# A hybrid encoder layer in which the first product starts block by block, neighbourhood attention takes two heads at a time, and the ends of two stages are rearranged

## The reference, cut to what matters

```python
h = rms_norm(x, norm_g)
dq, dk, dv, nq, nk, nv, gates = jnp.split(h @ w_in, IN_SPLITS, axis=-1)
y_diff = diff_attention(...)            # (p1 - lam * p2) @ v, per head, with a shared bias
y_na = neighborhood_attention(nq, nk, nv, rpb)   # per head and query: its window of keys, a bias per head
x = x + (g_diff * (y_diff @ w_br_diff) + g_na * (y_na @ w_br_na)) @ w_out
aff = softmax(rms_norm(x, norm2_g) @ w_router)
gate, idx = lax.top_k(aff.T, cap)       # 32 prompt and 64 sample tokens per expert
y = x + scatter_add((silu(xe @ wg) * (xe @ wu)) @ wd * gate)
```

## Time and profile before

| | us |
|---|---|
| median of 3 runs (2209.09 to 2210.94) | 2210.21 |
| the profiled execution | 2212.8 |
| its span, as the profile shows it | 2211.0 |
| PE busy in the span | 2128.8 (96%) |
| DVE busy | 1582.0 (72%) |
| ACT busy | 1370.8 (62%) |
| POOL busy | 238.7 (11%) |
| mean granted clock of TensorE | 0.987 |

### The profile page before, as it was taken

The page is one execution under the profiler, slowest core; times in us unless marked ns, Lnnn a source line. Parts: engine busy times, 40 slices in busy tenths (PEclk is TensorE's granted clock), DMA queues, the critical chain, the costliest instruction groups (busy, mean ns, idle before and its releaser), DMA issues.

```text
span 2211.0 us, 27257 instructions
## 1 busy us (share of the span) xinstructions
PE 2128.8 (96%) x10388; PEld 1592.4 (72%) x10388; DVE 1582.0 (72%) x1249; ACT 1370.8 (62%) x1102; POOL 238.7 (11%) x137
## 2 busy tenths in 40 slices
PE   6999999999968999999999999999999999999997
PEld 5867888887756767777677776767767677777765
DVE  5374363233456888888888888888888888888885
ACT  5364364122225777777777777777777777777764
POOL 2202120000130001010101102011010201101010
PEclk9999999999988999999999999999999999999999
DMA  5111141113436999999999999999999999999995
GB/s 232 58 36 67 58 144 60 64 58 115 162 118 236 373 370 366 376 371 385 364 368 385 367 378 370 373 373 370 378 365 380 365 374 385 367 376 374 375 372 184
DMA packets 71389, 623.97 MB, mean 282 GB/s; under 512 B 8272, under 2 KB 8656, under 8 KB 18608
## 3 DMA queue, kind: packets, MB, share of 16 engines
q1 hardware_dynamic: 63264, 595.62, 69.6%
q0 software_dynamic: 7648, 27.40, 4.4%
q10 hardware_dynamic: 432, 0.34, 0.0%
HBM read 609.70 MB, written 13.63 MB: 282 GB/s over the span
## 4 chain that ended last, share of the span: by engine, by line
PE 82%; DMA 7%; DVE 6%; ACT 4%; issue 1%; POOL 0%; ACTq 0%; SPq 0%; DVEq 0%; POOLq 0%
PE PS L527 25%; PE PS L529 25%; PE PS L528 25%; DMA x_w_raw<-in_w_expert_gate 5%; DVE x_w_low L1160 4%; ACT x_w_high L1090 3%; PE PS L625 2%; PE PS L610 2%; PE PS L872 1%; DMA x_w_raw<-in_w_expert_up 1%; PE PS L638 1%; PE PS L536 1%; PE PS L815 1%; PE PS L736 0%; DMA cst<-in_consts 0%
## 5 line engine op out<-in xcount | busy, mean ns | idle before, releaser
L1160 DVE TENSOR_TENSOR x_w_low<-x_w_raw,x_w_high 128x2048 fp32r<-128x2048 f32 (+1 forms) x382 | 1174.5, 3086 | 241.9 <-ACT x_w_high L1090 239.6
L1090 ACT ACTIVATE x_w_high<-x_w_raw 128x3072 fp32r<-128x3072 f32 (+1 forms) x384 | 980.0, 2558 | 266.2 <-PE PS L529 190.9
L527 PE MATMUL PS<-x_w_high,xT_high 128*96 128x512 f32 (+1 forms) x1536 | 580.5, 378 | 9.7 <-DVE x_w_low L1160 7.6
L529 PE MATMUL PS<-x_w_high,xT_low 128*96 128x512 f32 (+1 forms) x1536 | 575.4, 375 | 0.0
L528 PE MATMUL PS<-x_w_low,xT_high 128*96 128x512 f32 (+1 forms) x1536 | 573.4, 373 | 0.0
L527 PEld LDWEIGHTS PS<-x_w_high,xT_high 128*96 128x96 f32 x1536 | 248.3, 162 | 105.6 <-DVE x_w_low L1160 18.6
L529 PEld LDWEIGHTS PS<-x_w_high,xT_low 128*96 128x96 f32 x1536 | 248.1, 162 | 90.0
L528 PEld LDWEIGHTS PS<-x_w_low,xT_high 128*96 128x96 f32 x1536 | 248.8, 162 | 85.1 <-issue 0.2
L527 PE MATMUL PS<-x_w_high,hidden_high 128*96 128x512 f32 x704 | 281.3, 400 | 0.0
L529 PE MATMUL PS<-x_w_high,hidden_low 128*96 128x512 f32 x704 | 276.7, 393 | 0.0
L528 PE MATMUL PS<-x_w_low,hidden_high 128*96 128x512 f32 x704 | 275.9, 392 | 0.0
(11 more groups left out here) (185 smaller groups left out, 1774.4 us busy)
## 6 DMA issues: line engine op xcount, KB each, us to landing
x_w_raw<-in_w_expert_gate SPq DMA_DIRECT2D x96, 1536.0 KB, 8.4
x_w_raw<-in_w_expert_up SPq DMA_DIRECT2D x96, 1536.0 KB, 8.8
x_w_raw<-in_w_expert_down SPq DMA_DIRECT2D x96, 1536.0 KB, 8.3
x_w_raw<-in_w_expert_gate SPq DMA_DIRECT2D x32, 1024.0 KB, 7.5
x_w_raw<-in_w_expert_up SPq DMA_DIRECT2D x32, 1024.0 KB, 7.4
x_w_raw<-in_w_expert_down SPq DMA_DIRECT2D x32, 1024.0 KB, 7.0
w_raw<-in_w_in SPq DMA_DIRECT2D x20, 1024.0 KB, 4.8
x<-in_x_sample SPq DMA_DIRECT2D x8, 512.0 KB, 13.5
```

The lines of the kernel that those rows point to most:

```text
L527: mm(out, sh, mh, start=first, stop=False)
L529: return mm(out, sl, mh, start=False, stop=last)
L1090: a_(xh[:, w % SPLITS, 0:n], xraw[:, w % RAWS, 0:n], ACT.Copy).then_inc(x_high, 1)
L1160: return v.tensor_tensor(out, src, high.bitcast(F32), ALU.subtract)
```

## The change

What it does, in the order of the program:

- SP loads `rows` first and then block by block one `xT` block (384 KB) and one block of unit 0 (256 KB), four times; ACT and DVE split block by block too, and PE makes the products of unit 0 with the block as the outer loop. `cst` and the lambda vectors are loaded by POOL later, and PE waits for `cst` only behind unit 0.
- The lambda sums and their exponentials are moved into stage `pd`; the transposes of stage `pd` follow three products behind their tile (two before, `LAG`).
- In both attentions the last value product (tile 5) is made behind the first two logit steps, and DVE's copy of it (`keep_values`) stands behind the second bias step. The norms of `yd` are taken one tile earlier.
- Neighbourhood attention takes two heads in a step, as `diff` does: 24 steps, `kT` is one tensor with both heads in it, the zeroing is gone, logits are two products on half of the rows each, transposes and value products are four per step, the copy is one of 512 columns, the division by the sum is one DVE instruction of 128 columns. Sample bias tables have four buffers; heads 0 and 1 are loaded before stage `pn`'s norms.
- The last output unit has a raw buffer of its own (`w_last`) and no wait for a split; the residual rows `x` are loaded a stage part earlier.
- At the router's end POOL splits only expert unit 0; DVE takes unit 1, and does the gathered tokens' low parts and unit 1 ahead of the tables. PE no longer waits for the tables.

```diff
@@ -351,17 +353,26 @@
             def load_unit(n, src):
+                if n == UNITS - 1:
+                    stage_done(sp, 5)
+                    sp.dma_start(w_last, src.rearrange("p (k c) -> p k c", k=4)).then_inc(S("o", "last_unit_loaded"), 16)
+                    return
+                if n >= 2:
+                    sp.wait_ge(w_split, n - 1)
                 sp.dma_start(wraw[:, n % 2], src.rearrange("p (k c) -> p k c", k=4)).then_inc(w_loaded[n % 2], 16)

-            for u in range(2):
-                for i in (2 * u, 2 * u + 1):
-                    sp.dma_start(xT[:, 2 * i:2 * i + 2, :], x_turned[:, 2 * i:2 * i + 2, :]).then_inc(s_xT[i], 16)
-                load_unit(u, src_of("pd", "q", u))
+            sp.dma_start(rows, vectors).then_inc(s_rows, 16)
+            first = src_of("pd", "q", 0).rearrange("p (k c) -> p k c", k=4)
+            for k in range(4):
+                sp.dma_start(xT[:, k, :], x_turned[:, k, :]).then_inc(S("n1", f"xT_loaded{k}"), 16)
+                sp.dma_start(wraw[:, 0, k], first[:, k]).then_inc(S("n1", f"w_loaded{k}"), 16)
+            for i in range(2, 4):
+                sp.dma_start(xT[:, 2 * i:2 * i + 2, :], x_turned[:, 2 * i:2 * i + 2, :]).then_inc(s_xT[i], 16)
+            load_unit(1, src_of("pd", "q", 1))
             for t in range(NT):
                 sp.dma_start(xv[:, t, :], xsrc(x_prompt, x_sample, t)).then_inc(s_x[t], 16)
             for stage, kind, u0, nu in CHUNKS:
                 for u in range(max(u0, 2), u0 + nu):
-                    sp.wait_ge(w_split, u - 1)
                     load_unit(u, src_of(stage, kind, u - u0))
                 if kind == "gate_d0":

...
             def load_sample(h):

-                pool.wait_ge(S("na", "biased"), 4 * (h % 2) + 4 if h < 2 else 16 + 4 * (h - 1))
-                pool.dma_start(bias_w[:, h % 2, :], bias_sample[h]).then_inc(S("na", f"bias_sample{h % 2}"), 16)
-
+                if h >= 2:
+                    pool.wait_ge(S("na", "biased"), 2 * (h - 1) if h < 4 else 8 + 4 * (h // 2 - 1))
+                pool.dma_start(bias_w[h % 4], bias_sample[h]).then_inc(S("na", f"bias_sample{h % 4}"), 16)
+
+            pool.wait_ge(S("n1", "tev"), 4)
+            pool.dma_start(cst, consts).then_inc(s_cst, 16)
+            pool.dma_start(lamv, lambdas).then_inc(s_lamv, 16)
+            pool.wait_ge(S("n1", "tev"), KD)
             load_diff(0)
             load_diff(1)
...
+            load_sample(0)
+            load_sample(1)
...
-            for h in range(8):
+            for h in range(2, 8):
...
-            for w in range(2):
-                n = unit_width(w)
-                pool.wait_ge(x_high, w + 1)
-                nc.gpsimd.tensor_tensor(xl[:, w, 0:n], xraw[:, w, 0:n], xh[:, w, 0:n].bitcast(F32), ALU.subtract
-                                        ).then_inc(x_split, 1)
+            n = unit_width(0)
+            pool.wait_ge(x_high, 1)
+            nc.gpsimd.tensor_tensor(xl[:, 0, 0:n], xraw[:, 0, 0:n], xh[:, 0, 0:n].bitcast(F32), ALU.subtract
+                                    ).then_inc(x_split, 1)
...
-            pe.wait_ge(s_cst, 32)
...
-                    elif t == 0:
-                        pe.wait_ge(S("n1", "tev"), 4)
+
+                if before is None:
+
+                    for k in range(4):
+                        pe.wait_ge(S("n1", "tev"), k + 1)
+                        pe.wait_ge(S("n1", "w_low"), k + 1)
+                        for t in range(NT):
+                            i = split_product(PS[:, t, :], hTh[:, k, t * P:(t + 1) * P], hTl[:, k, t * P:(t + 1) * P],
+                                              wh[:, 0, k], wl[:, 0, k], k == 0, False)
+                            if k == 3:
+                                i.then_inc(w_prod, 1)
+                    pe.wait_ge(s_cst, 16)
...
-                    if before is None or n >= START_EARLY:
+                    if (NT if before is None else START_EARLY) <= n < len(steps) - 1:
                         chunk_product(chunks, c, u, t, hTh, hTl, bank_free)
-                    while jt < len(done_at) and n >= done_at[jt] + 2:
+                    while jt < len(done_at) and n >= done_at[jt] + LAG[stage]:
...
                 for step in range(len(L) + 5):
+                    if step == 2:
+                        chunk_product([c for c in CHUNKS if c[0] == stage], 2, 1, NT - 1, hTh, hTl, None)
                     if step < len(L):
-                        h, qt, t0, nt = L[step]
-                        ring = 4 // nm
-                        if step >= ring:
-                            pe.wait_ge(S(br, "biased"), step - ring + 1)
-                        for m in range(nm):
-                            c, r = (h, m) if br == "diff" else (h // 2, h % 2)
-                            half = slice(64 * r, 64 * r + 64) if br == "diff" else slice(None)
+                        c, qt, t0, nt = L[step]
+                        if step >= 2:
+                            pe.wait_ge(S(br, "biased"), step - 1)
+                        for r in range(2):
+                            half = slice(64 * r, 64 * r + 64)
                             queries = qT[half, c, (t0 + qt) * P:(t0 + qt + 1) * P]
-                            keys = kT[r][half, c, t0 * P:(t0 + nt) * P]
+                            keys = kT[half, c, t0 * P:(t0 + nt) * P]
                             if br == "na" and t0 == 2:
-                                keys = kT[r][:, c, SP_:N].rearrange("p (r c) -> p r c", c=GW)[
+                                keys = kT[half, c, SP_:N].rearrange("p (r c) -> p r c", c=GW)[
                                     :, :, WINDOWS[qt]:WINDOWS[qt] + 32]
-                            i = mm(PS[:, nm * (step % ring) + m, 0:nt * P], queries, keys, start=True, stop=True)
+                            i = mm(PS[:, 2 * (step % 2) + r, 0:nt * P], queries, keys, start=True, stop=True)
                         i.then_inc(S(br, "log"), 1)
                     a = step - 5
                     if 0 <= a < len(L):
...
                         w = P if br == "diff" else 64
+                        heads = [h] if br == "diff" else [2 * h, 2 * h + 1]
...
-                        for c in range(nt):
-                            values = vw[qt // 2][:, qt % 2, c, :] if windowed else vv[:, t0 + c, :]
-                            i = mm(PS[:, 6 + a % 2, 0:w], turned[:, a % 2, c * P:(c + 1) * P],
-                                   values[:, h * w:(h + 1) * w], start=c == 0, stop=c == nt - 1)
+                        for r, head in enumerate(heads):
+                            for c in range(nt):
+                                values = vw[qt // 2][:, qt % 2, c, :] if windowed else vv[:, t0 + c, :]
+                                i = mm(PS[:, 6 + a % 2, r * w:(r + 1) * w],
+                                       turned[:, a % 2, (r * nt + c) * P:(r * nt + c + 1) * P],
+                                       values[:, head * w:(head + 1) * w], start=c == 0, stop=c == nt - 1)
                         i.then_inc(S(br, "pv"), 1)
                     a = step - 3
                     if 0 <= a < len(L):
                         h, qt, t0, nt = L[a]
                         if a == 0:
                             pe.wait_ge(S(stage, "pused"), 3 * NT)
-                        pe.wait_ge(S(br, "probs"), a + 1)
+                        pe.wait_ge(S(br, "probs" if br == "diff" else "exp"), a + 1)
                         if a >= 2:
                             pe.wait_ge(S(br, "aT"), a - 1)
                         maps = sT if br == "diff" else s_na
-                        for c in range(nt):
+                        for c in range(nt if br == "diff" else 2 * nt):
                             i = nc.tensor.transpose(PS[:, 4 + a % 2, c * P:(c + 1) * P],
-                                                    maps[:, a % 4, 0, c * P:(c + 1) * P], ident)
...
-                act.wait_ge(s_xT[k // 2], 16)
+                act.wait_ge(*((S("n1", f"xT_loaded{k}"), 16) if k < 4 else (s_xT[k // 2], 16)))
                 a_(hTh[:, k, :], xT[:, k, :], ACT.Copy, scale=g1[:, k:k + 1]).then_inc(S("n1", "high"), 1)
-                if k % 4 == 3:
-                    split_units(k // 4 + 1)
+                if k < 4:
+                    act.wait_ge(S("n1", f"w_loaded{k}"), 16)
+                    a_(wh[:, 0, k], wraw[:, 0, k], ACT.Copy).then_inc(S("n1", "w_high"), 1)
+            unit[0] = 1
+            split_units(2)
             for t in range(NT):
...
-                if k % 4 == 3:
-                    split_units(k // 4 + 1)
+                if k < 4:
+                    dve.wait_ge(S("n1", "w_high"), k + 1)
+                    low(wl[:, 0, k], wraw[:, 0, k], wh[:, 0, k]).then_inc(S("n1", "w_low"), 1)
+            dve.wait_ge(S("n1", "w_low"), 4)
+            dve.sem_inc(w_split, 1)
+            unit[0] = 1
+            split_units(2)
             dve.wait_ge(S("n1", "sq"), NT)
...
-                        table = bias_of(br, h, t0, qt)[:, 0:n]
```

(20 more changed lines are left out.)

125 lines of the change are left out of this document (67 added, 58 removed).

## The result

The changed kernel takes 2191.86 us (median of 20 runs, 2185.57 to 2211.47) against 2210.26 (20 runs) of the kernel before: ratio 0.9939, 95% interval 0.9916 to 0.9961. It is faster by 0.6%, and by less than forecast: 2184.5 was said, 2177 to 2191 the range.

The account below looks back on a forecast made before the run. PE was taken to set the pace, the weight stream close behind, with gains only before the experts' loop. Terms 9.3 + 0.8 + 6.9 + 4.1 + 4.6 = 25.7 us gave 2187.1 profiled, 2184.5 as median; range 2177 to 2191.

Parts of the forecast that it names:

- The start: Program start: block-by-block loads and splits bring the first product at 7.9 instead of 17.2 us, 9.3 us gained.
- no wait above 1 us before 110: Sign to look for from the start on: PE waits nowhere longer than 1 us before 110 us.
- The zeroing [...]: nothing: Start: zeroing, lambda work and second key copy leave engines that had slack, so they gain nothing.
- Differential attention: Its start: the late value product covers the third logit step's wait for DVE's first bias, 0.8 us gained.
- Neighbourhood attention: Whole stage: 3.8 us from pairs, 1.1 from bias tables, 2.0 from the stage's start, 6.9 in sum, bounds 3 and 13.
- A pair has values 2 x 0.39 = 0.78: Neighbourhood attention: value products of a two-head step take 0.78 us, part of a pair's 1.94 us.
- the 2.0: Start of neighbourhood attention: one norm moved away and a value product in the gap gain 2.0 us (0 to 3.4).
- The output product: Last output unit: its earlier load removes PE's 2.6 us wait and some slow clock, 4.1 us gained (2.6 to 4.6).
- The router's end: Before the experts: 3.0 us from POOL splitting one part and 1.6 from reordered DVE work, 4.6 us gained.
- The experts: Experts' loop: its body is left alone and a raw unit's later load costs nothing, so no change.
- rival 4: Experts' loop: gives the router's 4.6 us back, with DMA engines at 95% and one load later: 2189; chance 0.05.
- rival 1: The clock: short PE pauses bring one or two more half-clock spells costing 2 to 5 us, 2187 to 2190; chance 0.15.

Follow-up runs that it names:

- experiment 2: Changed kernel with neighbourhood attention one head at a time again, zero-padded key copies included: 2198.38 us, ratio 0.9954 to the kernel before.
- experiment 4: Changed kernel with the last value product ahead of the attention again, in both branches: 2190.96 us, ratio 0.9917 to the kernel before.
- experiment 3: Changed kernel with full-row logits in the neighbourhood pairs: 2188.35 us; or with two pairs' half-row logits behind each other: 2192.33 us.
- experiment 1: Changed kernel run again without edit on three chips: 2188.24, 2193.24 and 2201.65 us.
- experiment 6: Changed kernel with the next unit's load held until the value windows landed: 2190.27 and 2190.38 us; with later window loads instead: 2191.05 us.
- experiment 7: Changed kernel with the last four value-window loads held until the eleventh pair's bias: 2217.2 us; the same with full-row logits: 2203.08 us.
- a_third: Changed kernel run again without edit, on another chip: 2193.24 us, ratio 0.9941 to the kernel before.
- warm_router: Changed kernel with extra products in PE's waits at the router's end: 2201.52 us, ratio 0.9945 to the kernel before.
- a_fourth: Changed kernel run again without edit, on a further chip, with a slow execution profiled: 2201.65 us, ratio 0.9951 to the kernel before.
- pause_full: Changed kernel with full-row neighbourhood logits and the last four value-window loads held until the eleventh pair's bias: 2203.08 us, ratio 0.9974 to the kernel before.
- double_logits: Changed kernel with the half-row logits of two neighbourhood pairs behind each other, every second step: 2192.33 us, ratio 0.9913 to the kernel before.
- best2: Changed kernel with the next unit's load behind the value windows, extra products at the router's end and doubled neighbourhood logits: 2191.56 us, ratio 0.9916 to the kernel before.

## Why the prediction was off, step by step

Two steps failed. The forecast held one or two more spells of low clock at 2 to 5 us and never asked when the value windows land; shown is a spell of 37.6 us that costs 17.8, with 19 of 47 runs in the upper group, 7 of them in the 20 whose median lies over the range. And it had a pair at 1.94 us, with its values at 0.78; shown are 2.11 and 0.95, or 24 x 0.17 = 4.1 us, where the sum as a whole was 3.2 too high.

- **The start** (9.3): 8.6 measured; 0.65 of the miss is the first block's landing, 4.55 instead of 3.9. The step that failed is "no wait above 1 us before 110": PE reached the first transposes 1.6 us before the scaled projection. The lag of three products did not cover the norms, for which the start now leaves less time. Both numbers are of one execution: in the four profiles of this kernel the first product is 7.7 to 8.6 us earlier, and the wait is 1.6, 0.6, 0.7 and under 0.3 us. "The zeroing [...]: nothing" held for the start before alone: behind the new one it would have cost some 3 us (experiment 2).
- **Differential attention** (0.8): from the wait behind the start to its last values 2.6 us. 2.0 of these are the half clock at 130 us: profiles of the same code have 73.2 us for this stage with that spell and 71.2 without. It comes and goes between executions. The early logits are 0.7 (experiment 4).
- **Neighbourhood attention** (6.9 = 3.8 + 1.1 + 2.0): 3.9 measured. "A pair has values 2 x 0.39 = 0.78" failed: behind half-row logits they take 0.95. I took the drain behind the logits to stand in their own 0.63 of the earlier trace rows; it lies in the product that follows. So the pairs give PE nothing in this stage (50.6 against 50.4), and the 3.9 come from its waits: PE's are 1.6 us in total instead of 4.8, near the 3.1 said for bias tables and stage start. The split is in part luck: the early logits, meant for the 2.0, are worth 0.5 to 0.9 (experiment 4). The Trainium skill, TensorEngine Tiling (Array Packing), section Key Properties, has changes of the tiling drain the engine; experiment 3 agrees, with 0.09 + 0.12 = 0.21 us a pair.
- **The output product** (4.1): 4.35. **The router's end** (4.6): 2.9 + 1.9 = 4.8. **The experts** (nothing): nothing beyond their scatter; rival 4 did not come.
- **The clock**: rival 1 had the mechanism and the wrong place and size ("One or two more spells cost 2 to 5 us", chance 0.15). I priced a spell from those of the kernel before, which end within 7 us (6.8 at 130 us, 3.4 at 567), and took 292 us, where 3.36 us of waiting left the clock up, as evidence against. Shown by experiments 1, 6 and 7: a pause within the half-row pairs can put the clock down, in the two profiles that caught this it did not come back until large products ran, and the rest of the stage costs 17.8 us. The step that let it in is missing from the prediction: I counted when the bias tables arrive, and not when the value windows do, the other transfer for which that stage waits; the sum has them at nothing without a word.

The Trainium skill, TensorE: Matmul & The Clock Gate, Part 1, has activity of the engine release the lower clock. By busy time the upper profile disagrees: from 308 to 344 us PE is busy for 36.00 of 36 us, at 0.50 throughout.

Open: why a wait of 1.7 us puts the clock down in one execution and waits of 2.1 us leave it up in two others (a_third, warm_router); why the clock comes back in doubled steps and not in pairs; why the chips differ (0 of 5 to 8 of 12); and what share of the windows' lateness is due to the bias tables' earlier loads, which was not tried.

## What to carry to other kernels

Before the gain of an earlier stage or of earlier tables is booked, list every transfer for which the stage waits, with its first issue, its first use and what else is on the way between them. Half-row products side by side save less than their overlap, since each change of tiling is paid at both ends, and in the pairs here they left the clock at 1.2 GHz once a pause had put it there. Full-row products cost PE the same (2.14 against 2.11 us a pair), and with them the clock came back; but to be right they need zero-padded keys, whose zeroing cost some 3 us where it stood ahead of the norms. What removed the low clock here was to remove the pause: let what the stage waits for land first. And when the times of a kernel fall into two groups, the mean clock of the span says which executions to profile.

## What the hardware showed unexpectedly

- TensorE stayed at 1.2 GHz for some 37.6 us (1.1 + 36 + 0.5 by the windows of a_fourth) while the profile has it busy without a gap, and rose only 3 us into the large products that fill the stage's tail.
- With full-row products of the same number it rose within 5 us of the pause's end (pause_full), and with doubled half-row steps within 4.2 us (double_logits) or after 24 (best2).
- The clock can fall just behind a short pause and not in it: 0.8 us after PE had gone on, behind 1.7 us of waiting (a_fourth).
- Two half-row products of 256 columns take 0.63 us against 0.87 for two full-row ones, and cost 0.09 us ahead and 0.12 behind.
